# A two-layer decoder trunk in split float32: two weight tensors moved by 64 bytes within the on-chip memory

## The reference

```
h = h + rglru_mixer(rmsnorm(h), ...)
h = h + (silu(hn @ w_gate) * (hn @ w_up)) @ w_down
h = h + swa_sink_mixer(rmsnorm(h), ...)
for e in range(8):
    out = out + comb[..., e:e+1] * swiglu(hn, w_gate[e], w_up[e], w_down[e])
h = h + out
return rmsnorm(h, norm_final)
```

## Time and profile before

| | |
|---|---|
| median of 3 runs | 1576.96 us (1574.61 to 1580.67) |
| the profiled execution | 1578.29 us, span 1576.5 us |
| busy: TensorE, VectorE, ScalarE, GpSimd | 96%, 74%, 58%, 1% of the span |
| TensorE clock granted, mean | 0.977 of 2.4 GHz |
| read from memory | 422.92 MB, 269 GB/s over the span |

### The profile page before, as it was taken

One profiled execution on the slowest core, in us unless ns is written; L12 is line 12 of the kernel. 1 busy time (PEld: TensorE's weight loads), 2 busy tenths in 40 slices (PEclk: granted clock), 3 DMA queues, 4 the chain that ended last, 5 costly groups with the idle time before them and its releaser, 6 DMA issues.

```text
span 1576.5 us, 25498 instructions
## 1 busy us (share of the span) xinstructions
PE 1513.4 (96%) x10707; PEld 1379.9 (88%) x10707; DVE 1165.8 (74%) x1169; ACT 908.5 (58%) x911; POOL 13.2 (1%) x19
## 2 busy tenths in 40 slices
PE   6999999999987999999999999999999999999995
PEld 4779999998977899889989989989989998998983
DVE  5554555556644888888888888788888878888883
ACT  2623433444432666767676666676676767766661
POOL 0000000003000000000000000000000000000000
PEclk9999999999998899999999999999999999999997
DMA  7336555553315699899999999989989989998900
GB/s 255 134 128 237 179 178 184 184 187 134 108 54 213 255 344 369 303 363 369 332 347 354 329 348 354 338 335 360 370 302 365 365 332 347 354 331 347 356 26 29
DMA packets 62330, 425.63 MB, mean 270 GB/s; under 512 B 8077, under 2 KB 10249, under 8 KB 11017
## 3 DMA queue, kind: packets, MB, share of 16 engines
q1 hardware_dynamic: 60240, 422.60, 72.7%
q10 hardware_dynamic: 1976, 1.39, 0.3%
HBM read 422.92 MB, written 1.05 MB: 269 GB/s over the span
## 4 chain that ended last, share of the span: by engine, by line
PE 90%; DVE 4%; ACT 2%; issue 1%; POOL 1%; DMA 1%; ACTq 0%; POOLq 0%; DVEq 0%
PE ps L1548 38%; PE ps L1570 20%; PE ps L1262 10%; PE ps L1284 5%; PE ps L1186 4%; PE ps L1518 2%; PE ps L1536 2%; PE ps L1330 2%; PE ps L1433 2%; PE ps L1555 1%; DVE w_lo L1056 1%; ACT w_hi L584 1%; PE ps L1377 1%; PE ps L1177 1%; POOL hn L1162 0%
## 5 line engine op out<-in xcount | busy, mean ns | idle before, releaser
L1056 DVE TENSOR_TENSOR w_lo<-ring,w_hi 128x2048 fp32r<-128x2048 f32 x336 | 766.6, 2290 | 138.6 <-ACT w_hi L584 134.4
L584 ACT CAST w_hi<-ring 128x2048 fp32r<-128x2048 f32 x336 | 641.3, 1914 | 274.2 <-PE ps L1548 224.5
L1548 PE MATMUL ps<-w_hi,xg_hi 128*96 128x256 f32 x1792 | 251.0, 282 | 2.5 <-ACT w_hi L584 2.5
L1548 PE MATMUL ps<-w_lo,xg_hi 128*96 128x256 f32 x1792 | 247.3, 280 | 0.8
L1548 PE MATMUL ps<-w_hi,xg_lo 128*96 128x256 f32 x1792 | 247.4, 281 | 0.0
L1548 PEld LDWEIGHTS ps<-w_hi,xg_hi 128*96 128x96 f32 x1792 | 225.3, 162 | 15.6 <-issue 2.6
L1548 PEld LDWEIGHTS ps<-w_lo,xg_hi 128*96 128x96 f32 x1792 | 220.3, 162 | 2.4 <-DVE w_lo L1056 2.4
L1548 PEld LDWEIGHTS ps<-w_hi,xg_lo 128*96 128x96 f32 x1792 | 221.2, 163 | 0.0
L787 DVE TENSOR_TENSOR w_lo<-ring,w_hi 128x2048 fp32r<-128x2048 f32 x52 | 119.2, 2294 | 87.0 <-ACT w_hi L484 87.0
L484 ACT CAST w_hi<-ring 128x2048 fp32r<-128x2048 f32 x52 | 98.8, 1902 | 123.4 <-PE ps L1262 101.7
L1570 PE MATMUL ps<-w_hi,ht_hi 128*96 128x512 f32 x448 | 128.2, 408 | 0.0
(11 more groups left out here) (254 smaller groups left out, 1384.7 us busy)
## 6 DMA issues: line engine op xcount, KB each, us to landing
ring<-in_moe_w_gate SPq DMA_DIRECT2D x112, 1024.0 KB, 5.4
ring<-in_moe_w_up SPq DMA_DIRECT2D x112, 1024.0 KB, 5.7
ring<-in_moe_w_down SPq DMA_DIRECT2D x112, 1024.0 KB, 5.4
ring<-in_ffn_w_gate SPq DMA_DIRECT2D x14, 1024.0 KB, 4.8
ring<-in_ffn_w_up SPq DMA_DIRECT2D x14, 1024.0 KB, 4.9
ring<-in_ffn_w_down SPq DMA_DIRECT2D x14, 1024.0 KB, 4.8
ring<-in_lru_w_in SPq DMA_DIRECT2D x8, 1024.0 KB, 8.1
ring<-in_attn_w_qkv SPq DMA_DIRECT2D x6, 1024.0 KB, 4.9
```

The source lines that it names most:

```text
L584: nc.scalar.copy(w_hi[:, (SPLITS + n) % PARTS], ring[:, s]).then_inc(hi_done, 1)
L1056: V.tensor_tensor(w_lo[:, part], ring[:, ORDER_MOE[n % SLOTS]], w_hi[:, part].bitcast(F32), ALU.subtract).then_inc(lo_done, 1)
L1548: mm = nc.tensor.matmul(ps[0:CAP, c % 2, m * CHF:(m + 1) * CHF], xs[a][:, k], w[b][:, k], start=(k == 0 and (a, b) == (0, 0)), stop=(k == ...
```

## The change

Two small tensors of 16 float32 (64 bytes) are declared, one between ring and w_hi and one between w_lo and h. Nothing reads or writes them.

```diff
         ring = sb("ring", [P, SLOTS, SLOT])
+        gap = sb("gap", [P, 16])
         w_hi, w_lo = sb("w_hi", [P, PARTS, SLOT], F32R), sb("w_lo", [P, PARTS, SLOT], F32R)
+        gap2 = sb("gap2", [P, 16])
         h = sb("h", [P, KC, T])
```

## The result

The changed kernel takes 1561.45 us (median of 4 runs, 1557.86 to 1563.36) against 1578.12 us before (median of 4 runs, one more than in the table ahead), a ratio of 0.9893 with a 95% interval of 0.9865 to 0.9921.

The account below looks back on a forecast made before the run. TensorE was taken as the bound, streaming one column a cycle with no other time in it. All four parts were priced 0, so the forecast was the median of the runs before, 1577 us, range 1566 to 1594.

Parts of the forecast that it names:

- Steps 1 and 2: ScalarE's casts to w_hi and VectorE's subtractions to w_lo: the shifted addresses cost neither any time, price 0.
- Step 4: Tensors behind w_lo, shifted by 128 bytes: same residue mod 128, output DMA still 2.6 us, taken at 0.
- Step 3: TensorE's matmul reads of shifted w_hi and w_lo: price 0, bounded above by 1.7 ns or, far away, 13.3 ns.
- Rival 1: Every matmul on w_hi or w_lo slower: 15 us at 4 cycles each (1592 us), or up to 1677 us; chance 0.17.
- Rival 3: Experts' down product loses its unexplained 7.5 ns per matmul: 10 us faster, 1567 us, -0.6%; chance 0.05.
- Rival 2: Conversions outgrow their cover: VectorE's subtractions over 2.6 us each, at 2.9 us +102 us, 1679 us; chance 0.04.
- rival 4: The change does not do what it says, an allocator rounding the starts: same time; chance 0.02.

Follow-up runs that it names:

- run 1: Against the kernel before: w_hi and w_lo unmoved, only the 128-byte shift of everything behind w_lo is left; 1577.23 us, ratio 1.0006.
- run 4: Against the kernel before: w_hi, w_lo and everything behind them moved by 128 bytes; 1573.19 us, ratio 0.9971.
- run 8: The change, plus zero_mem 64 past a multiple of 128, with what lies behind it moved by 256 bytes; 1553.43 us, ratio 0.9835.
- Runs 2: The change without its second unused tensor: w_hi, w_lo and everything behind them 64 past a multiple of 128; 1560.34 us, ratio 0.9903.
- runs 3: The change without its first unused tensor: w_hi and w_lo as before, everything behind them 64 past a multiple of 128; 1568.44 us, ratio 0.995.
- 10: Against the change: w_hi stays at 64, w_lo goes back to 0 past a multiple of 128, all behind moved by 256 bytes; 1568.84 us, ratio 0.9942.
- Runs 6: Against the change: w_hi and w_lo 32 past a multiple of 128 instead of 64, all behind as in the change; 1570.17 us, ratio 0.9948.
- 7: Against the change: w_hi and w_lo 96 past a multiple of 128 instead of 64, all behind as in the change; 1575.65 us, ratio 0.9986.
- 5: Layout of before: from the fourth piece on, casts and subtractions convert only 16 of 2048 columns, all waits stay; 1561.3 us in a single execution.
- run 11: As run 8, with the hidden values ht_hi and ht_lo at 64 past a multiple of 128 too; 1556.72 us, ratio 0.986.

## Why the prediction was wrong

*Steps 1 and 2* (casts and subtractions, price 0) hold: 1909 and 2290 ns against 1914 and 2290. The pairs of the earlier trace rows read the two engines rightly.

*Step 4* (the shift of what lies behind, 0) holds by run 1, 1.0006, with one limit that run 4 and run 8 show: 128 bytes matter where w moves by them against an operand that stays, and 64 bytes matter for zero_mem, whose four matmuls come just ahead of others. The output's DMA still takes 2.6 us.

*Step 3* (TensorE's reads, price 0) is the step that failed. Measured, it is -6.6 and then -2.2 ns for a matmul in the FFN; in gate and up about -2 ns on the mean (5.46 or 5.62 us for 48 against 5.60 or 5.68); and about +1 ns in the down product (2.79 to 2.81 us for 12 against a mixture with 2.77). That is 5.3 us less in the FFN and 8.4 in the experts (about 10 from gate and up, less some 2 for the down product); 2.3 us more went between the stages. It rested on the sum that fitted: 256 + 128/4 = 288 cycles and 256 + 96/4 = 280. The fit was taken for the bare cost of the work and holds at one placement only: with the operands 64 apart, 128 stationary columns come down to 113.3 ns, 272 cycles, and 96 to nearly the same, 5.46/48 = 113.8 ns, so that the term for the stationary columns is gone. A pace that is exact and constant had been read as a pace without a stall; it held 16 cycles in each FFN matmul that another place saves. The bound below 0 was there ("less than that if ..."), but was tied to the down product only, and the bound should have been the distance to 256 cycles, 13 ns per FFN matmul.

*Rival 1* (slower, each matmul pays) named the right place and, but for the down product's 1 ns, the wrong sign. Its argument against itself, that two levels of pace at the same addresses come from timing and not from place, is where the reading went astray: they come from both. Runs 2 and 8 have the same w and u as the change and another pace, and runs 3 and 10 have another pace by place. The two levels in the earlier trace rows were the sign that the pace holds more than columns; they were priced as a nuisance of 3 us.

*Rival 3* (faster, 0.05) had a mechanism of this kind, reads that are parted by a shift, and the wrong product: the down product got slower, and its unexplained 7.5 ns stay unexplained. It also took 5.60 us as the floor of a gate-and-up stretch, where 5.46 was to be had.

*Rival 2 and rival 4* are out: no conversion grew, and the addresses did what they say.

The Trainium skill ("SBUF — State Buffer", Specifications) was used for a 0 from 16-byte lines. Runs 6, 7 and the change differ by whole lines of 16 bytes and differ in time (1570, 1576 and 1561 us), so the number of lines touched does not tell a matmul's pace. The Trainium skill ("TensorE: Matmul & The Clock Gate", Step-by-step: what each phase is for) calls TensorE's two read ports for the streaming operand and for the weight load independent. If that is read as saying that the place of one against the other costs nothing, it does not hold here: from before to run 8 an FFN matmul goes from 120.0 to 113.3 ns, 6.7 less, and run 3 gives some of the experts' stretches 2.9 ns a matmul by moving the tokens alone. The measurement decides.

What stays open: whether it is a matmul's own stationary load or the next one's that meets the stream; why 64 bytes is the best distance of those tried; what fixes the phase behind L1298 and in the experts, where half of the chunks stay at 5.62; and where the down product's 1 ns comes from. The runs show that these places act, not by which circuit.

## What to carry to other kernels

Where TensorE is the bound and every matmul loads new stationary data, the place of the two operands relative to each other is worth a trial, here of 32 to 128 bytes: it costs a line, and here it gave 1.1% at 64, and 1.65% with a second tensor moved. Compare the step from matmul to matmul with the bare count of moving columns before calling a stream stall-free; a constant excess is still an excess. Judge such trials by the pace of each product in the chain, since totals of different causes agree by chance (runs 2, 5 and the change all lie near 1561 us).

## What was not expected of the hardware

- With 256 moving columns the step between matmuls was 120.0, 118.7, 118.3, 117.8 or 113.3 ns in the FFN, by placement alone, at a granted clock of 1.00.
- At one and the same placement two paces can be stable, 113.3 and 117.8 ns, each for hundreds of matmuls; four matmuls of 0.96 us in all, on an operand moved by 64 bytes, chose between them (run 8), and in run 11 the slow one came first and the fast one behind those four.
- In the FFN a distance of 128 bytes is not the same as 0: 118.7 against 120.0 ns (run 4).
